# Layer two's router: where its squares stand, when two weight loads are issued, and what two others wait for

## The reference

```python
x = x + gt1 * latent_mixer(...)             # its last product is merged @ w_out
h2 = modulate(rmsnorm(x, g_ffn[l]), sh2, sc2)
x = x + gt2 * expert_choice_ffn(h2, ...)

def expert_choice_ffn(h, w_router, w_g, w_u, w_d):
    logits = einsum('bnd,de->ben', h, w_router)
    aff = softmax(logits, axis=1)
    gate, idx = top_k(aff, cap)             # 16 experts choose 64 of 512 tokens each
    xs = h[bi, idx]
    a = einsum('becd,edf->becf', xs, w_g)   # 1024 x 1024 weights for each expert, three times
    u = einsum('becd,edf->becf', xs, w_u)
    y = einsum('becf,efd->becd', silu(a) * u, w_d)
    return zeros_like(h).at[bi, idx].add(y * gate[..., None])
```

## Time and profile before

| | |
|---|---|
| median of 3 runs | 3042.7 us (3042.65 to 3042.92) |
| the profiled execution | 3041.93 us, of which its span is 3039.8 us |
| granted TensorE clock, mean | 0.994 |
| PE busy | 2926.5 us, 96% of the span |
| DVE, ACT, POOL busy | 1115.6, 622.8, 78.3 us |
| DMA | 587.50 MB, mean 193 GB/s |

### The profile page before, as it was taken

The page is one execution under the profiler, slowest core; times in us unless marked ns, Lnnn a source line. Parts: engine busy times, 40 slices in busy tenths (PEclk is TensorE's granted clock), DMA queues, the critical chain, the costliest instruction groups (busy, mean ns, idle before and its releaser), DMA issues.

```text
span 3039.8 us, 33448 instructions
## 1 busy us (share of the span) xinstructions
PE 2926.5 (96%) x13265; PEld 1464.3 (48%) x13265; DVE 1115.6 (37%) x1678; ACT 622.8 (20%) x1157; POOL 78.3 (3%) x92
## 2 busy tenths in 40 slices
PE   7999999999999999999999999999979998999999
PEld 4565655555555222222234655677433333334547
DVE  4764546566614000000147554334121110138352
ACT  3145530000002110101022453111011101021161
POOL 1000000000000001102000000000000000000000
PEclk9999999999999999999999999999989999999999
DMA  8230013443523899999971201223489999974300
GB/s 256 66 94 15 15 38 129 174 165 125 165 78 111 355 374 396 368 401 349 364 208 38 80 28 30 74 83 90 180 337 417 418 418 418 418 227 114 83 1 28
DMA packets 252321, 587.50 MB, mean 193 GB/s; under 512 B 64280, under 2 KB 143912, under 8 KB 231048
## 3 DMA queue, kind: packets, MB, share of 16 engines
q1 hardware_dynamic: 237072, 554.02, 49.4%
q0 software_dynamic: 7680, 22.62, 2.5%
q10 hardware_dynamic: 7416, 8.71, 1.2%
HBM read 561.44 MB, written 15.21 MB: 190 GB/s over the span
## 4 chain that ended last, share of the span: by engine, by line
PE 87%; DMA 7%; DVE 3%; issue 1%; ACT 1%; SPq 1%; ACTq 0%; DVEq 0%; POOL 0%; POOLq 0%
PE ps L1076 26%; PE ps L1527 10%; PE ps L1651 7%; PE ps L1539 5%; PE ps L1141 5%; PE ps L1096 5%; PE ps L1191 5%; PE ps L1367 3%; PE ps L1355 3%; PE ps L1401 3%; PE ps L1204 2%; PE ps L1588 2%; PE ps L1165 2%; DMA ring<-in_w_e_up 1%; DMA ring<-in_w_e_down 1%; PE ps L1341 1%
## 5 line engine op out<-in xcount | busy, mean ns | idle before, releaser
L1076 PE MATMUL ps<-hT,ring 128*128 128x512 f32 (+1 forms) x1696 | 604.5, 514 | 3.5 <-ACT hT L1889 3.4
L1076 PEld LDWEIGHTS ps<-hT,ring 128*128 128x128 f32 x1696 | 321.9, 191 | 276.0 <-issue 251.9
L1527 PE MATMUL ps<-ring,hT 128*64 128x512 f32 x992 | 235.9, 605 | 3.0 <-DMA ring<-in_w_e_up 3.0
L1141 PE MATMUL ps<-hT,ring 128*128 128x512 f32 (+1 forms) x448 | 181.5, 533 | 0.7 <-DVEq L1874 0.7
L1651 PE MATMUL ps<-ring,hT 128*64 128x512 f32 x640 | 157.6, 602 | 17.4 <-DMA ring<-in_w_e_down 10.0
L1889 ACT ACTIVATE prob<-prob,nms 128x768 f32<-128x768 f32 (+5 forms) x224 | 159.2, 711 | 14.9 <-DVE nms L2582 4.5
L1191 PE MATMUL ps<-merged,ring 128*128 128x512 f32 (+1 forms) x384 | 142.7, 526 | 3.1 <-issue 3.1
L1367 PE MATMUL ps<-con,prob 128*128 128x128 f32 x872 | 140.1, 283 | 3.5 <-DVE merged L2606 1.6
L1076 PE MATMUL ps<-obuf,ring 128*128 128x512 f32 (+1 forms) x384 | 142.1, 523 | 0.0
L1367 PEld LDWEIGHTS ps<-con,prob 128*128 128x128 f32 x872 | 96.4, 140 | 91.8 <-issue 78.8
L1889 ACT ACTIVATE prob<-ps 128x768 f32<-128x768 f32 (+2 forms) x55 | 36.7, 667 | 490.7 <-PE ps L1076 418.9
(11 more groups left out here) (368 smaller groups left out, 3675.1 us busy)
## 6 DMA issues: line engine op xcount, KB each, us to landing
ring<-in_w_e_gate SPq DMA_DIRECT2D x79, 1024.0 KB, 15.4
ring<-in_w_e_up SPq DMA_DIRECT2D x65, 1024.0 KB, 14.4
ring<-in_w_e_down SPq DMA_DIRECT2D x60, 1024.0 KB, 13.5
ring<-in_w_in SPq DMA_DIRECT2D x49, 1024.0 KB, 6.1
ring<-in_w_ada SPq DMA_DIRECT2D x48, 1024.0 KB, 6.7
merged<-in_w_e_up SPq DMA_DIRECT2D x25, 1024.0 KB, 14.8
merged<-in_w_e_down SPq DMA_DIRECT2D x19, 1024.0 KB, 12.6
merged<-in_w_e_gate SPq DMA_DIRECT2D x18, 1024.0 KB, 16.0
```

The costliest lines, as they stand in the source:

```text
L1076: mm = pe.matmul(ps[:, b + a:b + e], lhs[:, k, :], rhs[:, k, a:e], start=k == 0, stop=k == nk - 1)
L1141: mm = pe.matmul(ps[:, BANK[SIDE]:BANK[SIDE] + hi - lo], ring3(slot)[:, k, m % 2 * P:(m % 2 + 1) * P], h3[:, k, lo:hi], start=k == 0, stop ...
L1527: mm = pe.matmul(ps[e * CX:(e + 1) * CX, b + h * 512:b + (h + 1) * 512], lhs, second_weights(slot_of[sub], e, h), start=k == 0, stop=k == ...
```

## The change

For layer two the first square stays in `qbuf[0:512]`, and the others go to four buffers in `hT[0:2048]`, the first part of h, which no product reads after the gates. With this, loads 9 and 23 no longer touch a buffer of squares: they wait for the last branch product instead of the last addition of squares, and SP issues them in the list of loads that are issued ahead. SP's order becomes 0, 1, 2, 9, 15, 19, 23, 27, 38, then 3 to 8, 10, the four stores of token tiles, 11, 12, 13, 14, 16 and so on. Loads 12 and 13 wait for `chosen_ready` alone, no longer for the gathered rows to land.

```diff
--- before.py
+++ after.py
@@ -226,8 +226,7 @@
         def square_of(l, d):
             if l == 0:
                 return h3[:, d, :]
-            at = 0 if d == 0 else 1 + (d - 1) % 4
-            return qbuf[:, at * NX:(at + 1) * NX] if at < 2 else kbuf[:, (at - 2) * NX:(at - 1) * NX]
+            return qbuf[:, 0:NX] if d == 0 else hT[:, (d - 1) % 4 * NX:((d - 1) % 4 + 1) * NX]
@@ -1698,16 +1697,13 @@
                     pass
                 elif slot == IN_XT:
                     sp.wait_ge(hpre.sem, hpre.at[1, "mix", KD - 1, NX])
-                elif slot == IN_KQ or slot == GAPS:
-                    sp.wait_ge(acc_ready.sem, acc_ready.at[1, "x"])
                 elif slot == MIDDLE - 1:
                     sp.wait_ge(xw_ready.sem, xw_ready.at["wout", 1, KD - 1, "x"])
                 elif slot == MIDDLE:
                     sp.wait_ge(rows_written[1, "x"], 64)
                 elif MIDDLE < slot <= SCRATCH:
                     sp.wait_ge(chosen_ready.sem, chosen_ready.at[1, "x"])
-                    sp.wait_ge(rows_landed[1, "x"], 32)
-                elif slot >= RING:
+                elif slot >= RING or slot == GAPS:
                     sp.wait_ge(gate_used.sem, gate_used.at["branch", 1, 1, KD - 1])
@@ -1744,15 +1740,13 @@
             end = LOOPC[0] + RING
             for n in range(end, LOOPC[1] + EARLY):
                 load(n)
-            later = ONCE_AT.index(23)
-            for r in ONCE_AT[:later] + ONCE_AT[later + 1:]:
+            ahead = ONCE_AT + tuple(second_first[GAPS + n] - LOOPC[1] for n in range(1))
+            for r in sorted(ahead):
                 load(LOOPC[1] + r)
             for n in range(LOOPC[1] + EARLY, len(chunks)):
-                if second_first.get(MIDDLE - 1) == n:
-                    load(LOOPC[1] + ONCE_AT[later])
                 if second_first.get(MIDDLE) == n:
                     write_rows(1, "x", 0, 4)
-                if n - LOOPC[1] not in ONCE_AT:
+                if n - LOOPC[1] not in ahead:
                     load(n)
```

## The result

The changed kernel took 3047.45 us, the median of 20 runs (3043.57 to 3049.22), against 3042.68 us for the kernel before (20 runs, 3040.33 to 3046.29). The ratio is 1.0015, with a 95% interval of 1.0008 to 1.0022: slower by 2.4 to 6.7 us, about 4.8. The forecast was 3044.4, its range 3040.7 to 3047.0; the time lies 0.45 us above that range. The profiled execution took 3046.94 us, its span 3044.8, against 3041.93 and 3039.8.

A forecast was written before the change was run, and what follows sets the result against it. Layer two's experts were taken as bound by their bytes, with load 14 tied to step 0's end. Profiled 3041.9 + 2.1 (gather late) - 0.4 = 3043.6, or 3044.4 beside the median of 3042.7; range 3040.7 to 3047.0.

The forecast's parts named there:

- What bounds the kernel: Layer two's experts end when their bytes have come; load 14, first into a used place, is tied to step 0's end.
- Rival 2: Loads moved from busy to idle DMA time save 5.0 us per pair, giving 3037.7 or 3032.7; chance 0.10.
- Price 0: Loads 9 and 23 issued ahead, and squares moved into h, were each forecast to cost nothing.
- the upper bound: Delay of PE's start on gathered rows if loads 12 and 13 move first: 2.1 us, taken as the cost.
- the late end: Of a gather delay between 0 and 2.1 us, the forecast took 2.1 us.
- the reading by equal turns: Gather gets half the DMA rate, 209 GB/s, beside loads 12 and 13: cost 0.9 us, sum 3043.2.
- 128 GB/s from 2230 on: Gather's assumed rate beside loads 12 and 13, under a third of the engines, taken from a later gather.
- PE's gap 3.8 us: Forecast gap from the four clock-holding matmuls to the first piece on PE, up from 1.7 us.
- a rival with a chance of 0.10: PE's clock falls while it waits for the gather, adding 1.9 us, for 3046.3; chance 0.10.
- first steps at half clock: Sign that the forecast is wrong: the first expert steps run with PE's clock at half.
- 1.9 us: Forecast price of PE's clock falling: half the work lost over some 3.8 us.
- The gain of 0.4: Loads 12 and 13 out earlier remove bytes still on their way at 2242, worth 0.4 us.

The follow-up runs named there:

- e1: Changed kernel, but loads 12 and 13 wait for the gathered rows again; 3043.91 us, ratio 1.0000 to the kernel before.
- e12: Kernel before with six clock-holding matmuls instead of four; 3042.81 us, ratio 0.9999.
- e9: Kernel before with only load 13, no longer load 12, held for the gathered rows; 3044.00 us, ratio 1.0004.
- e5: Changed kernel with load 13 alone held for the gathered rows, load 12 still in front; 3042.35 us, ratio 0.9996 to the kernel before.
- e8: Changed kernel with load 13 held until the first of the two gathers lands; 3045.19 us, ratio 1.0004 to the kernel before.
- e11: Changed kernel with load 13 held for both gathers and six clock-holding matmuls instead of four; 3042.04 us, ratio 0.9997 to the kernel before.
- e3: Changed kernel with eight clock-holding matmuls instead of four; 3044.62 us, ratio 1.0010 to the kernel before.
- e10: Changed kernel with load 13 held for the first gather and six clock-holding matmuls instead of four; 3044.09 us, ratio 1.0001 to the kernel before.
- e4: Changed kernel with loads 12 and 13 released by POOL's signal instead of `chosen_ready`; 3049.73 us, ratio 1.0022 to the kernel before.
- e2: Kernel before with one edit: loads 12 and 13 no longer wait for the gathered rows; 3047.78 us, ratio 1.0017.

## Why the prediction was wrong

**What bounds the kernel: right.** In every kernel of the table load 14 goes out within 0.1 us of step 0's end, and the stretch behind it runs at 417 or 418 GB/s. Rival 2, bytes that count wherever they are moved, is refuted: e1 has two loads moved out of the busy time and is at 1.0000.

**Loads 9 and 23, squares: right.** Price 0, by e1, within its interval of 2.7 us. In the trace after, the squares and their additions take 0.63 and 0.69 us as before. Load 11 went out 9.1 us ahead of the numbers instead of 3.2, as the row stores ended sooner, and the gather, which waits for the numbers, had none of it.

**The gather: delay right, price too small.** 2.1 us was called the upper bound; it was 3.0. The step that failed is the working of that bound, which let loads 12 and 13 begin 1.2 us after the numbers and gave all bytes 418 GB/s from the first one on. In the trace after, they do begin within 1.2 us, but the first two microseconds carry 49 and 147 GB/s and the next seven some 380 on average, so the 3.15 million bytes need until 2238.7, 9.8 us from the numbers and not 8.75. A bound from a steady rate isn't one for a burst of 3 MB. The choice of the late end was right, and the reading by equal turns was not (0.9 us). But the way there was not the one of the forecast, which gave the gather 128 GB/s from 2230 on: it had nothing for 4.5 us and then about half. The rule of the Trainium skill ("DMA: Bandwidth & Descriptors", section "Queues, rings and completion order"), turns between queues that have work, agrees with the packets of 2235 to 2237, 0.44 against 0.38 MB. It says nothing of the time before: up to 2234 SP's queue moved alone, and whether the gather had packets ready by then no run here shows.

**The clock: the failure that cost the range.** The forecast itself made PE's gap 3.8 us, and then left the falling clock to a rival with a chance of 0.10. The rows gave 1.7 us as borne and 5 us as not, and 3.8 us is nearer to the second. It should have stood in the sum, or had a chance far above 0.10. The prediction named first steps at half clock as a sign that it was wrong, and the trace after shows it: 0.50 through most of step 0. Its price was also too small: 1.9 us was taken from the warm-up of the holding matmuls, while step 0 took 2.7 us longer. The sum with the measured terms, 3.0 + 2.7 = 5.7 us to load 14, stands beside 4.8 us (2.4 to 6.7) measured.

**The gain of 0.4: not shown.** Between the two profiles the rest, from load 14 to the end of the last step, fell from 453.8 to 451.8 us, which looks like 2 us given back. But that rest lies between 451.8 and 454.5 in all 13 profiles, and not by the order of the loads: e12, with the order of the kernel before and load 14 at nearly the same point, has 452.0, and e1 454.5. SP begins to issue the last two loads 31.2 us before the end in 12 of the 13 (31.8 in e9), so the difference arises in the full DMA stretch ahead of them. What sets it is open, and so is whether an early load 12 or 13 is worth anything.

## What to carry to other kernels

A wait that keeps bulk loads behind a gather is worth its idle DMA time where the gather starts the next stage and the loads have no use before it; a load of 1 MB in front made the rows 0.2 to 0.9 us late here (e5, e8 to e11), two 3.0 or more. When a wait of TensorE grows, price the clock with it: here it nearly doubled the delay of step 0's end (2.7 us on 3.0). Give the fall a chance of its own in the sum, taken from gaps that the trace shows, and not a small one where the gap is nearer to one that fell. Freed time in a transfer queue brought nothing that shows here while the next transfer waited for a buffer; look for the first load that takes a used place, and count from what releases it.

## What the runs showed of the hardware

The clock's fall was less regular than the gaps suggest. In the profiles the holding matmuls were followed by gaps of 1.51, 1.65, 1.70 and 1.75 us with the clock kept (e1, e5, before, e3), and it fell after 2.40, 2.63, 4.08, 4.20, 4.71 and 6.76 us, but also after 1.35 and 0.84 us (e10, e11). So for one execution the length of the gap alone doesn't tell. Nor does what PE did between the holding matmuls and step 0, where it also waits between the pieces. From 2234 to 2237 in e11 it is busy for 0.15, 0.72 and 0.60 us, and the clock falls as step 0 begins; from 2236 to 2239 in e5 it is busy for 0.00, 0.56 and 0.50 us, and the clock stays up through step 0. The price of a fall in step 0 was 1.3 to 2.7 us.

The clock also goes with the spread between runs of one kernel, 4 to 7 us here: the 33 runs of the kernel before beside e1 to e4 take 3041.6 us on average where the mean granted clock is 0.995, 3042.7 at 0.994 and 3044.1 at 0.993. That is a correlation; no profile shows where in those runs the clock was low.

The second surprise is how unequal two megabytes are. In the kernel before the gather's first packet moved 1.5 us behind its issue, with one load in front some 3 us (e5, e8 to e11), with two 4.1 to 4.5 (changed, e2, e3, and e4, where SP issued them just behind the first gather). Behind one load (e5) it then had the DMA engines alone and made up nearly all of it; behind two (changed) it shared them with what was left of the second, and the rows were 3.0 us late.
